# Key tiles around the maxima of the gated memory, and two steps of VectorE exchanged

## The reference, cut to what matters

```python
# 1. gated delta rule, 6 heads x 2 directions, chunks of 64 tokens
a = jnp.where(strict, einsum('bhnld,bhnsd->bhnls', kb, k) * lmask, 0.0)
t = lax.linalg.triangular_solve(a + eye, eye, lower=True, unit_diagonal=True)
u = einsum('bhnls,bhnse->bhnle', t, v * beta[..., None])
wk = einsum('bhnls,bhnsd->bhnld', t, kb * exp(gc)[..., None])

# 2. gated memory (mLSTM), 4 heads x 2 directions: running maxima keep its exponentials in range
dmat = where(causal, bcum[..., :, None] - bcum[..., None, :] + ig[..., None, :], -inf)
m_t = maximum(max(dmat, axis=-1), bcum + m_prev[..., None])
s_intra = einsum('bhnld,bhnsd->bhnls', q, k) * exp(dmat - m_t[..., None])

# 3. keys and values of the cross attention, from the other input "mem" (256 x 1024)
kk, vv = jnp.split(rmsnorm(mem, w) @ w_kv, 2, axis=-1)
```

## Time and profile before

| | |
|---|---|
| time, median of 3 runs | 1035.52 us (1034.82 to 1035.82) |
| the profiled execution's own time | 1036.81 us |
| its span, first to last instruction | 1035.1 us |
| TensorE busy | 1017.3 us, 98% |
| VectorE busy | 748.5 us, 72% |
| ScalarE busy | 571.4 us, 55% |

### The profile page before, as it was taken

The page is one execution under the profiler, slowest core; times in us unless marked ns, Lnnn a source line. Parts: engine busy times, 40 slices in busy tenths (PEclk is TensorE's granted clock), DMA queues, the critical chain, the costliest instruction groups (busy, mean ns, idle before and its releaser), DMA issues.

```text
span 1035.1 us, 21287 instructions
## 1 busy us (share of the span) xinstructions
PE 1017.3 (98%) x8907; PEld 928.9 (90%) x8907; DVE 748.5 (72%) x1192; ACT 571.4 (55%) x843; POOL 70.9 (7%) x177
## 2 busy tenths in 40 slices
PE   9999999999999999999999999998999999999997
PEld 8778999999987899999998888968899899998885
DVE  5879687788867966778799876766787566555445
ACT  4775586454666558544467674234345456675333
POOL 8600000000000000002140000000000000000000
PEclk9999999999999999999999998999999999999999
DMA  9656554455664555348778440101355356565652
GB/s 324 180 176 186 144 163 133 142 169 175 195 184 126 162 143 161 107 144 250 180 190 208 124 148 23 65 22 43 119 178 173 124 158 179 173 183 188 197 185 82
DMA packets 73551, 160.54 MB, mean 155 GB/s; under 512 B 6917, under 2 KB 16320, under 8 KB 73456
## 3 DMA queue, kind: packets, MB, share of 16 engines
q1 hardware_dynamic: 70304, 150.59, 47.6%
q0 software_dynamic: 2832, 8.06, 4.0%
q10 hardware_dynamic: 320, 0.53, 0.1%
HBM read 158.11 MB, written 1.05 MB: 154 GB/s over the span
## 4 chain that ended last, share of the span: by engine, by line
PE 90%; DVE 4%; ACT 3%; DMA 2%; issue 1%; SPq 0%; POOL 0%; ACTq 0%; DVEq 0%; POOLq 0%
PE psum L472 24%; PE psum L474 24%; PE psum L473 23%; PE psum L891 2%; DMA ring<-in_w_in 2%; PE psum L1037 2%; PE psum L880 1%; PE psum L732 1%; PE psum L710 1%; DVE ring_lo L1443 1%; ACT ring_hi L2511 1%; DVE arena L1629 1%; PE psum L1363 1%; PE psum L724 1%; PE psum L1380 1%
## 5 line engine op out<-in xcount | busy, mean ns | idle before, releaser
L1443 DVE TENSOR_TENSOR ring_lo<-ring,ring_hi 128x1024 fp32r<-128x1024 f32 (+4 forms) x291 | 342.4, 1194 | 163.0 <-ACT ring_hi L2511 161.4
L2511 ACT ACTIVATE ring_hi<-ring 128x1024 fp32r<-128x1024 f32 (+4 forms) x291 | 297.7, 1034 | 249.1 <-PE psum L474 228.1
L472 PE MATMUL psum<-hT,ring_hi 128*128 128x256 f32 x904 | 258.4, 286 | 0.0
L474 PE MATMUL psum<-hT,ring_lo 128*128 128x256 f32 x904 | 254.9, 282 | 0.0
L473 PE MATMUL psum<-hT,ring_hi 128*128 128x256 f32 x904 | 254.5, 282 | 0.0
L472 PEld LDWEIGHTS psum<-hT,ring_hi 128*128 128x128 f32 x904 | 171.6, 190 | 2.4 <-issue 1.0
L473 PEld LDWEIGHTS psum<-hT,ring_hi 128*128 128x128 f32 x904 | 171.6, 190 | 0.0
L474 PEld LDWEIGHTS psum<-hT,ring_lo 128*128 128x128 f32 x904 | 171.6, 190 | 0.0
L472 PE MATMUL psum<-ring_hi,hT 128*128 128x512 f32 (+4 forms) x416 | 156.4, 376 | 2.8 <-DVE ring_lo L1443 2.2
L474 PE MATMUL psum<-ring_hi,hT 128*128 128x512 f32 (+4 forms) x416 | 151.9, 365 | 0.0
L473 PE MATMUL psum<-ring_lo,hT 128*128 128x512 f32 (+4 forms) x416 | 151.6, 364 | 0.0
(11 more groups left out here) (461 smaller groups left out, 1346.3 us busy)
## 6 DMA issues: line engine op xcount, KB each, us to landing
ring<-in_w_in SPq DMA_DIRECT2D x104, 512.0 KB, 3.6
ring<-in_w_ff SPq DMA_DIRECT2D x64, 512.0 KB, 3.6
ring<-in_w_branch SPq DMA_DIRECT2D x24, 512.0 KB, 3.4
ring<-in_w_out SPq DMA_DIRECT2D x24, 512.0 KB, 3.5
ring<-in_w_in SPq DMA_DIRECT2D x24, 384.0 KB, 3.3
ring<-in_w_xkv SPq DMA_DIRECT2D x16, 512.0 KB, 3.7
ring<-in_w_in SPq DMA_DIRECT2D x8, 528.0 KB, 4.0
ring<-in_w_xq SPq DMA_DIRECT2D x8, 512.0 KB, 3.9
```

The source lines that it names most:

```text
L472: mm(b, lhs[0], rhs[0], start=start, stop=False, **how)
L474: return mm(b, lhs[1], rhs[0], start=False, stop=stop, **how)
L1443: V.tensor_tensor(chunk_view(ring_lo, RAW, c), chunk_view(ring, RAW, c), plain(chunk_view(ring_hi, RING_HI, c)), ALU.subtract).then_inc(ev ...
L2511: AC(chunk_view(ring_hi, RING_HI, c), chunk_view(ring, RAW, c), ACT.Copy).then_inc(ev("whi_ready"), 1)
```

## The change

On TensorE, behind level 1: the heads' turns move ahead of the memory's maxima; one key tile goes between the two and one behind the maxima. In exchange level 2 has one key tile in its second place instead of two, and the single tile behind level 2 is gone. After level 2, four tiles are done in either version. On VectorE the lower part of weight chunk 38 (`lo_until(39)`) moves from ahead of `memory_low(0)` and `memory_low(1)` to behind them. ScalarE's program stays as it is.

```diff
@@ TensorE @@
             inverse_level(1, lambda: next(last_columns), lambda: memory_turns(2))
             memory_turns(3)
+            window_heads()
+            tiles(keys, 1)
             memory_maxima()
-            window_heads()
+            tiles(keys, 1)
...
-            inverse_level(2, one_tile, two_tiles)
-            one_tile()
+            inverse_level(2, one_tile, one_tile)
             inverse_level(3, one_tile, two_tiles)
             one_tile()
             memory_scores()
@@ VectorE @@
             inverse_start(0)
             lo_until(38)
             inverse_start(1)
-            lo_until(39)
             memory_low(0)
             memory_low(1)
+            lo_until(39)
             running_maxima()
             window_mask(0)
             inverse_level(1, 0)
```

## The result

The changed kernel takes 1039.85 us (median of 7) against 1035.52 (median of 7 as well). The medians lie 4.3 apart; the measured ratio is 1.0037 (that of the two medians alone would be 1.0042), with a 95% interval from 1.0026 to 1.0048. It is slower, by some 3.8 us, and lies above the forecast range.

The account below looks back on a forecast made before the run. TensorE, busy 1017.3 of 1035.1 us, was taken as the bound. The terms summed to -0.74 without a clock fall; one fall added 1.43, so +0.7 on 1035.52 gave 1036.2 us, range 1033.5 to 1038.3.

Parts of the forecast that it names:

- VectorE's exchange: Line 1114's wait for VectorE's `memory_low` (line 1914): 0.73 of its 1.1 us saved, bounds 0 and 1.1.
- The split pair: Key tiles: a pair takes 1.63 us, a tile alone 0.91; one pair is split, costing 0.19 us.
- the wait ahead of line 1024: Memory's maxima: new TensorE wait for ScalarE's copy of the first heads' turns, +0.66 us, range 0.4 to 1.0.
- Level 4: Level 4's first `tx` waits for VectorE to free a bank of `mqk`: +1.1 us, bounds 0.5 and 1.4.
- level 5: Level 5's first `tx` waits for VectorE to free a bank of `mu`: +0.5 us, bounds 0.2 and 0.7.
- the factors: Delta rule's `gw` and `gu2` fall on banks ScalarE reads one copy later: +0.8 us, bounds 0.3 and 1.0.
- The clock, if it doesn't fall: Line 1024, heads' turns and level 2's `tx`: 6.82 us at the lower clock avoided, -3.3 us.
- One more fall of 2.99: Clock falls once more near line 1024's end, for 2.99 us, costing 1.43 us.
- The first: Rival: the clock holds around the memory's maxima; -0.74, 1034.8 us; chance 0.27.
- The second: Rival: clock falls at the maxima and stays low as long as now, 6.82 us; +2.52, 1038.0 us; chance 0.17.
- The third: Rival: the clock holds and the later banks are free in time; -3.1, 1032.4 us; chance 0.13.
- The fourth: Rival: turns don't count for the clock, which falls 1.1 before line 1024's end; +1.7, 1037.2 us; chance 0.05.

Follow-up runs that it names:

- e1: Kernel before with VectorE's exchange alone (lower part of chunk 38 behind the two `memory_low`): 1034.90 us, 0.9996 of the kernel before.
- e11: Changed kernel with only the later PSUM banks dealt as in the kernel before, from behind level 2's `tx` on: 1036.62 us, 1.0010 of the kernel before.
- e3: Changed kernel with five weight chunks transferring only 16 of their 512 columns: 1038.58 us, 1.0029 of the kernel before.
- e4: Kernel before with the same five weight chunks cut to 16 of 512 columns: 1033.59 us, 0.9975 of the kernel before.
- e6: Changed kernel with PSUM banks moved so that all from the memory's scores on have the kernel before's readers: 1037.53 us, 1.0014 of the kernel before.
- e2: Kernel before with TensorE's new order alone, VectorE as before: 1042.39 us, 1.0058 of the kernel before.
- e7: Changed kernel with the tile ahead of the maxima moved between lines 1018 and 1024, and later banks as in the kernel before: 1037.54 us, 1.0019 of the kernel before.
- e10: e11 with the weight chunks of levels 1, 3 and 4 (and the two behind level 4's) held back: 1034.64 us, 0.9990 of the kernel before.
- e9: Kernel before with VectorE's exchange and the weight chunks of levels 1 and 4 (and the two behind) held back: 1032.49 us, 0.9964 of the kernel before.

## Why the prediction was wrong

- *VectorE's exchange, -0.73.* Right: the wait fell from 1.14 to 0.49, and e1 without a fall is 0.7 faster. Not foreseen: in e1's trace the earlier TensorE only reached a late piece of its program sooner.
- *The split pair (+0.19) and the wait ahead of line 1024 (+0.66).* The wait is 0.77, for the copy that was named. The terms of its working as listed (0.90, 0.11, 0.49 and twice 0.1) add up to 1.70 and not 1.6, which would have given 0.80. That the turns themselves would wait for a bank, 0.16 for `memory_low`, was not counted.
- *Level 4 (+1.1), level 5 (+0.5), the factors (+0.8).* The waits are 0.8, 1.6 and 0.7, where some 1.3, 1.5 and 0.7 were forecast; level 4's is smaller since a stall of 0.8 in level 3 had already held TensorE. e11 took these three away and gained 1.6 without a fall, two thirds of the 2.4 summed, while stalls took their place (`issue` 3.3 there).
- *Sum without the clock.* These terms add up to +2.52; the table gives 1036.8 less 1034.2, 2.6. That match is in part luck. The stalls were put at nothing, without a reason; by e3 and e4 they cost the kernel before some 2.7 and the changed one some 1.7, and with short chunks the two lie 3.6 apart. And the two profiled executions alone, taken without their falls, give 2.97 + 3.26 - 1.43 = 4.80 for the stretch: the single pair bears the sum out less well than the means do. Counted from line 1105, level 3's `tx` starts 31.7 later (at 649.04), where it was 32.7: 1.0 earlier, not 1.7 to 3.2, mainly for the stall in level 1, 0.78 where it was 0.27.
- *The clock: the step that failed.* "The clock, if it doesn't fall: -3.3" took the 6.82 of one profiled execution for what every execution loses. One more fall of 2.99, booked at +1.43, then left a gain of 1.83. In the profiled execution that second half came out to the hundredth: `tx` 2.33 against 1.57, and the tile behind it 1.58 (642.04 to 643.62) against 0.91, 1.43 together. That is luck: the fall came 1.4 behind the end of line 1024 and not at it, and 3.41 at 0.42 each stand in for 2.99 at 0.48. But over the executions the kernel before loses only some 3 low us, about half of what I booked as saved, and the changed one some 6, twice what I forecast. The second part goes with the later bank waits: it is gone in the mean where the banks are mended (e6, e11), and e2's trace has falls just behind such waits. So the clock's term is, in the mean, +1.4 in place of -1.83, and that error of 3.2 is the miss: 1036.2 and 3.2 make 1039.4. The warning was in the text: the profiled execution took 1.3 more than the median. I let "a difference carries over" stand, though the term that made it slow was the one I was about to subtract. By its own signs of being wrong, a missing wait or a clock that holds, the forecast would have looked right: all of them go by one profile.
- *Rivals.* The first, that the clock holds, did not come about: it fell in the profile, and none of the seven executions lists more than 0.997. The second, "low as long as now", came nearest, but by another way: not one longer fall in line 1024, but, in the mean, more of them. The third, later banks free in time, is refuted. The fourth, that the turns don't count, can't be the cause of the difference: e11 has the same turns at the same place and the mean low time of the kernel before.

What stays open: what makes the clock fall in one execution at the maxima and not in the next of the same program, and why a fall follows a wait of 1.0 at line 880 in e2's trace, and none the wait of 1.4 at the same place in the kernel before's. And with 5 to 12 executions of each kernel the low times are good to about 1 us only; e7 and e10, in between, can't be placed.

## What to carry to other kernels

Before a stretch at the lower clock is booked as a gain, look at the mean granted clock of several executions: a profile is one draw, and if it is slower than the median, the fall may be why. When steps on TensorE change places, replay the PSUM banks to the end of the stage, since waits far behind the edit can be most of its price, first as waits and then as clock. Where TensorE runs many small products, look for `issue` behind weight transfers, and hold back transfers that aren't needed yet.

## What the runs showed of the hardware

A piece of TensorE's program came at the very end of a weight chunk (2.4 to 2.7 long) three times in these traces: at 628.40 and 650.26 in the changed kernel, at 629.07 in e1. The stalls behind are 0.2 to 1.1, and with short chunks they are nearly gone (0.6 and nothing). Moving three chunks of 0.52 MB by some 6 to 19 us, with nothing else changed but a fourth that came some 2 us later, is worth about 2.5 us (e9 against e1, without a fall). And the same program loses between nothing (0.999) and some 3.5 us (0.995) to the clock from one execution to the next.
